# S5 output turned back in three parts, its input asked for one block earlier, and the squares of the second norm made per block

## The reference

```
u = rmsnorm(h);  z = u @ w_in                       # columns shared out to three mixers and gates
y_gla = (gated linear attention * silu(gate)) @ w_gla_out
s = per group of 16 channels: 64-dim complex state, associative scan over positions
s = gelu(C x + d * u);  s = s * sigmoid(s @ w_glu)   # S5 mixer: the "gated unit"
y_s5  = (s * silu(s_gate)) @ w_s5_out
y_att = (sliding-window attention * silu(a_gate)) @ w_attn_out
h = h + (g0*y_gla + g1*y_s5 + g2*y_att) @ w_out      # g = sigmoid(merge gates of u)
```

## Time and profile before

| | us |
|---|---|
| three timed runs | 1935.65, 1940.91, 1940.92 |
| profiled execution | 1936.7 (span of its trace 1934.8) |
| PE busy | 1774.6 (92%) |
| DVE busy | 969.9 (50%) |
| POOL busy | 782.0 (40%) |
| ACT busy | 694.5 (36%) |

### The profile page before, as it was taken

The page is one execution under the profiler, slowest core; times in us unless marked ns, Lnnn a source line. Parts: engine busy times, 40 slices in busy tenths (PEclk is TensorE's granted clock), DMA queues, the critical chain, the costliest instruction groups (busy, mean ns, idle before and its releaser), DMA issues.

```text
span 1934.8 us, 29460 instructions
## 1 busy us (share of the span) xinstructions
PE 1774.6 (92%) x12239; PEld 1588.4 (82%) x12239; DVE 969.9 (50%) x1527; ACT 694.5 (36%) x1236; POOL 782.0 (40%) x478
## 2 busy tenths in 40 slices
PE   6976898999998997989998999989999899799997
PEld 5876798999988996988997977777788687678886
DVE  8996134333429882467653203533333698635223
ACT  3453432444533221332324543344455221223322
POOL 2644665333323322533331786544332322334442
PEclk8898999999999998999998999999999999999999
DMA  9455244222254544535552333532223655523432
GB/s 146 142 164 152 79 104 117 81 68 66 65 146 142 181 138 100 104 82 177 157 163 85 99 87 88 132 93 77 76 61 72 176 172 179 110 77 98 140 101 87
DMA packets 356043, 221.77 MB, mean 115 GB/s; under 512 B 49604, under 2 KB 346744, under 8 KB 353352
## 3 DMA queue, kind: packets, MB, share of 16 engines
q1 hardware_dynamic: 345384, 189.75, 37.5%
q10 hardware_dynamic: 10528, 30.15, 4.6%
HBM read 172.17 MB, written 38.50 MB: 109 GB/s over the span
## 4 chain that ended last, share of the span: by engine, by line
PE 63%; DVE 10%; DMA 8%; POOL 6%; SPq 6%; ACT 4%; issue 3%; ACTq 0%; DVEq 0%; POOLq 0%
PE ring L794 45%; DMA sb_w_raw<-in_w_in 4%; POOL sb_w_lo L650 3%; PE ring L775 3%; PE ring L753 2%; PE aux L1037 2%; PE aux L1129 2%; DVE sb_s_prod L1515 1%; DVE sb_s_mat_prod L1515 1%; SPq L559 1%; DMA sb_w_raw<-in_w_s_out 1%; PE aux L1116 1%; SPq L525 1%; SPq L606 1%; DVE sb_s_gelu_lo L1515 1%
## 5 line engine op out<-in xcount | busy, mean ns | idle before, releaser
L650 POOL TENSOR_TENSOR sb_w_lo<-sb_w_raw,sb_w_hi 128x1024 fp32r<-128x1024 f32 x246 | 607.0, 2470 | 1067.3 <-ACT sb_w_hi L1181 1065.1
L1181 ACT ACTIVATE sb_w_hi<-sb_w_raw 128x1024 fp32r<-128x1024 f32 x246 | 259.9, 1057 | 654.5 <-DMA sb_w_raw<-in_w_in 409.6
L794 PE MATMUL ring<-sb_u_hi,sb_w_hi 128*128 128x264 f32 (+1 forms) x2112 | 358.7, 322 | 21.3 <-ACT sb_att_q L1223 11.0
L794 PEld LDWEIGHTS ring<-sb_u_hi,sb_w_hi 128*128 128x128 f32 x2112 | 304.8, 196 | 52.6 <-ACT sb_att_q L1223 12.6
L794 PE MATMUL ring<-sb_u_lo,sb_w_hi 128*128 128x264 f32 (+1 forms) x2112 | 338.4, 311 | 0.0
L794 PE MATMUL ring<-sb_u_hi,sb_w_lo 128*128 128x264 f32 (+1 forms) x2112 | 334.5, 309 | 0.0
L794 PEld LDWEIGHTS ring<-sb_u_lo,sb_w_hi 128*128 128x128 f32 x2112 | 298.5, 191 | 21.7
L794 PEld LDWEIGHTS ring<-sb_u_hi,sb_w_lo 128*128 128x128 f32 x2112 | 294.0, 188 | 21.1
L1213 ACT ACTIVATE sb_tmp_act<-ring 128x528 f32<-128x528 f32 (+1 forms) x112 | 67.5, 602 | 143.8 <-PE ring L794 103.3
L1437 ACT ACTIVATE sb_att_scores<-sb_att_scores,sb_att_neg_max 128x208 f32<-128x208 f32 x128 | 58.5, 458 | 90.8 <-DVE sb_att_neg_max L1800 90.8
L794 PE MATMUL ring<-sb_y_hi,sb_w_hi 128*128 128x264 f32 (+1 forms) x504 | 88.1, 325 | 3.2 <-ACT sb_w_hi L1181 3.1
(11 more groups left out here) (320 smaller groups left out, 2591.6 us busy)
## 6 DMA issues: line engine op xcount, KB each, us to landing
sb_w_raw<-in_w_in SPq DMA_DIRECT2D x166, 512.0 KB, 4.1
sb_s_loaded<-s_matrices ACTq DMA_DIRECT2D x16, 1808.0 KB, 7.5
s_matrices<-sb_s_phase SPq DMA_DIRECT2D x16, 528.0 KB, 3.2
s_matrices<-sb_s_mbt SPq DMA_DIRECT2D x16, 512.0 KB
s_matrices<-sb_s_ca SPq DMA_DIRECT2D x16, 512.0 KB
sb_w_raw<-in_w_gla_out SPq DMA_DIRECT2D x16, 512.0 KB, 4.1
sb_w_raw<-in_w_attn_out SPq DMA_DIRECT2D x16, 512.0 KB, 4.0
sb_w_raw<-in_s_w_glu SPq DMA_DIRECT2D x16, 512.0 KB, 4.2
```

Of the source, the lines that this page charges most:

```text
L650: pool.tensor_tensor(WL[:, w], WR[:, w], WH[:, w].bitcast(F32), ALU.subtract).then_inc(lo_ready, 1)
L794: last = pe.matmul(RING[:, 2 * r + hf, 0:c1 - c0], w[:, n % SLOTS, kt, :], moving(b[0], xx[:, kt], c0, c1), start=(term == 0 and kt == 0), ...
L1181: act.activation(WH[:, w], WR[:, w], ACT.Copy).then_inc(hi_ready, 1)
```

## The change

Four edits in one diff.

1. The S5 input is wanted behind block i = 2 instead of 3 (S5_IN = 2), and all 16 DMAs into Z4 are issued in SP's turn of ag 0. The scan of tile 0 moves up by one block with it. The places of the outputs, S5_OUT, keep their values.
2. The S5 output comes back in three parts, tiles 0 to 3, 4 and 5, 6 and 7, by 16 DMAs each, in SP's turns of i = 14, 18 and 21. Its target is a buffer of its own, YZ, in the room of the attention queries. ScalarE copies the first two parts in its turn of i = 20 and the third in that of i = 21; VectorE's subtractions follow in its turns of 21 and 22. GH moves to the room of Z. glu 0 runs alone (`project_as_made`), glu 1 by `project`.
3. The matrices of layer 1 lie elsewhere, and `input_matrix(1)` and `s5_matrices(1, 0)` are generators in two pieces each, run behind sg 2, 3, 4 and 5. The turn in which its C tiles are turned moves from sg 5 to sg 2.
4. In layer 0, ScalarE squares tile kt of the new h in the turn of wout kt + 1, into a buffer SQ of eight tiles in the room of UH. GpSimd adds tiles 1 to 6 to tile 0, behind its weight split of ga. TensorE sums that and tile 7 (`norm_sum_added`).

The core of the diff:

```diff
-S5_IN = 3
-S5_OUT = {S5_IN + 3 + 2 * j: j for j in range(KT)}
-S5_YT, S5_SPLIT = 21, 22
+S5_IN = 2
+S5_OUT = {6 + 2 * j: j for j in range(KT)}
+S5_YT = {14: (0, 4), 18: (4, 6), 21: (6, 8)}
+S5_SPLIT = {21: ((0, 4), (4, 6)), 22: ((6, 8),)}
+YT_PARTS = list(S5_YT.values())
...
-MATS_1 = [("sg", 5)] + [("ws5", j) for j in (0, 1, 2, 3, 5)] + [("wout", j) for j in (0, 2, 4)]
+MATS_1 = [("sg", 2)] + [("ws5", j) for j in (0, 1, 2, 3, 5)] + [("wout", j) for j in (0, 2, 4)]
...
-        GH = sb("s5_gelu_hi", [P, KT, L], F32R, at=[o_aq, o_aq + WIDE])
+        GH = sb("s5_gelu_hi", [P, KT, L], F32R, at=[base, base + WIDE])
+        YZ = sb("s5_out", [P, KT, STRIDE, STEPS], at=[o_aq, o_aq + WIDE])
...
-                    if name in (("ag", 0), ("ag", 1)):
-                        for q in (2 * name[1], 2 * name[1] + 1):
+                    if name == ("ag", 0):
+                        for q in range(QUADS):
...
-                    if name == S5F[S5_YT]:
-                        aux_read(sp, ly, ("y", 6))
-                        aux_read(sp, ly, ("y", 7))
+                    if name in S5F and S5F.index(name) in S5_YT:
+                        j0, j1 = S5_YT[S5F.index(name)]
+                        aux_read(sp, ly, ("y", j1 - 2))
+                        aux_read(sp, ly, ("y", j1 - 1))
                         for q in range(QUADS):
                             for t in range(STRIDE):
-                                sp.dma_start(Z[32 * q:32 * q + 32, :, t, :],
-                                             Z4[32 * t:32 * t + 32, :, q, :]).then_inc(yt_loaded, 16)
+                                sp.dma_start(YZ[32 * q:32 * q + 32, j0:j1, t, :],
+                                             Z4[32 * t:32 * t + 32, j0:j1, q, :]
+                                             ).then_inc(yt_loaded[YT_PARTS.index((j0, j1))], 16)
...
+                    if ly and b == 0:
+                        for kt in range(1, KT - 1):
+                            pool.wait_ge(sq_ready, KT + kt + 1)
+                            pool.tensor_tensor(SQ[:, 0], SQ[:, 0], SQ[:, kt], ALU.add).then_inc(sq_added, 1)
+                            pool.wait_ge(sq_added, kt)
...
+            def norm_sum_added(ly):
+                h = aux_take(ly, ("norm", 0))
+                for kt in (0, KT - 1):
+                    if kt:
+                        pe.wait_ge(sq_ready, KT * ly + KT)
+                    else:
+                        pe.wait_ge(sq_added, KT - 2)
+                    for hf, c0, c1 in column_parts(0):
+                        last = pe.matmul(AX_[:, 2 * h + hf, 0:c1 - c0], ONES[:], SQ[:, kt, c0:c1],
+                                         start=(kt == 0), stop=(kt == KT - 1))
+                last.then_inc(aux_full[h], 1)
...
-                project_two_as_made(ly, (("glu", 0), ("glu", 1)), GH, GL, ylo_ready, 32 * ly + 16)
-                for j in range(2, KT):
+                project_as_made(ly, ("glu", 0), GH, GL, ylo_ready, 32 * ly + 16)
+                for j in range(1, KT):
                     project(ly, ("glu", j), GH, GL)
...
+            def wout_squares(kt):
+                evacuated(act, 0, ("wout", kt))
+                act.activation(SQ[:, kt], H[:, kt], ACT.Square).then_inc(sq_ready, 1)
...
+                    if kind == "wout" and ly == 0 and j:
+                        wout_squares(j - 1)
...
-                            zs = [Z[:, j].rearrange("p s c -> p (s c)") for j in range(KT)]
-                            if i == S5_SPLIT:
-                                act.wait_ge(yt_loaded, 256 * ly + 256)
-                                for j in range(KT):
-                                    act.activation(GH[:, j], zs[j], ACT.Copy).then_inc(yhi_ready, 1)
+                            if i + 1 in S5_SPLIT:
+                                act.wait_ge(x_state, 8 * ly + 8)
+                                for part in S5_SPLIT[i + 1]:
+                                    act.wait_ge(yt_loaded[YT_PARTS.index(part)], 256 * ly + 256)
+                                    for j in range(*part):
+                                        act.activation(GH[:, j], YZ[:, j].rearrange("p s c -> p (s c)"), ACT.Copy
+                                                       ).then_inc(yhi_ready, 1)
...
-                    if ly == 0 and b == ("sg", 3):
-                        input_matrix(1)
+                    if ly == 0 and b == ("sg", 2):
+                        first_set = itertools.chain(input_matrix(1), s5_matrices(1, 0))
+                    if ly == 0 and kind == "sg" and 2 <= j <= 5:
+                        next(first_set)
...
-                            if i == S5_SPLIT:
-                                for t in range(KT):
+                            for part in S5_SPLIT.get(i, ()):
+                                for t in range(*part):
                                     dve.wait_ge(yhi_ready, 32 * ly + 16 + t + 1)
-                                    tt(GL[:, t], Z[:, t].rearrange("p s c -> p (s c)"), GH[:, t].bitcast(F32),
+                                    tt(GL[:, t], YZ[:, t].rearrange("p s c -> p (s c)"), GH[:, t].bitcast(F32),
                                        ALU.subtract).then_inc(ylo_ready, 1)
```

65 lines of the change are left out of this document (42 added, 23 removed).

## The result

The changed kernel takes 1917.61 us, median of four runs (1911.0 to 1920.78), the kernel before 1938.74 beside it (four runs): a ratio of 0.9891, 95% interval 0.9869 to 0.9912. That is 21 us of the 42 forecast, and outside the range on its slow side. The profiled execution took 1920.78 (span 1919.0), and TensorE is about as busy as before in less time (1778.7 us, 93%, by its page).

What follows compares the result with a forecast made beforehand. The prediction took the chain of waits as the bound, 63% of it on TensorE. A 12, B 27, C 1 and D 2 summed to 42 us off 1936.7, giving 1895 us, range 1878 to 1911.

Steps and rivals of the forecast that it cites:

- B: S5 output in three parts, glu 0 alone: TensorE's wait ahead of the gated unit shrinks; gain taken as 27 us.
- Cost nothing: Weight loads of blocks 17 and 21, behind the DMAs of parts 0 and 1, still reach TensorE in time: no loss.
- A: S5 input one block earlier: the first scan starts sooner and stalls at weights and first state go; taken 12 us.
- The new stall at ag 4's take: In layer 0, block 4's take, queued behind the first scan's second half, makes TensorE wait 3.6 us for block 6.
- its upper end: A with every VectorE operation at its undisturbed length: neither layer stalls, together a gain of 22 us.
- The second rival: In the first scan, block 4's take comes as late as the state did: A 0, gain 30, 1907 us; chance 0.10.
- the four subtractions in A's window: GpSimd's weight subtractions beside the first scan keep stretching VectorE's work, so the new stall of 3.6 us stays.
- C: First matrix set in four pieces behind sg 2 to 5: the stall is cut in two; gain taken as 1 us.
- D: Second norm with eight matmuls instead of 32, behind GpSimd's adds, ends earlier; gain taken as 2 us.
- The fourth rival: SP falls behind its weight loads at parts 0 and 1, stalling TensorE: slower, up to 1983 us; chance 0.07.

Runs made afterwards that it cites:

- b_off: The changed kernel with the S5 output moved by 16 DMAs at block 21 again and the first two gated unit blocks computed together: 1930.24 us, ratio 0.996.
- tanh_first: The changed kernel with ScalarE's tanh and y_hi in the turn of ag 1 ahead of the weight copy of ag 3: 1913.65 us, ratio 0.9879.
- half4_only: The changed kernel with the first scan's second half on VectorE behind the take of ag 4 instead of ag 3: 1914.31 us, ratio 0.9879.
- pool_small: The changed kernel with GpSimd subtracting only the first of eight pieces of each weight block in the S5 stage: 1883.84 us, ratio 0.9727.
- a_off: The changed kernel with 8 S5 input DMAs at ag 0 and 8 at ag 1 again, first state inputs behind ag 3: 1916.93 us, ratio 0.9896.
- cd_off: The changed kernel with the first matrix set behind sg 3 and sg 5 again and 32 matmuls in the second norm: 1917.56 us, ratio 0.9896.
- p01_adds: The changed kernel with output parts 0 and 1 behind their turn's weight load and four of GpSimd's six adds in wout: 1905.14 us, ratio 0.9831.

## Why the prediction was wrong, step by step

- **B, the waits: right.** Forecast a start after 2.2 us, measured 2.24, and 1.98 where 2.5 was forecast, behind GpSimd's rest of glu 0. The exact 2.2 is luck: the 16 issues took 10.65 us, 0.67 each, where I had taken 0.60, 1.05 us more in all, and the weights were split 4.7 us behind their issue (744.63 to 749.30) instead of 5.74, 1.1 less; layer 0's other two profiles have 1.69 and 2.84. The Trainium skill's rule on small transfers (DMA: Bandwidth & Descriptors, "Rules for kernel authors") gives no issue time, but it points the right way: a quarter of the bytes took the issue only from 0.72 to 0.67, and half of them (part 0, 11.35 us) to 0.71. Waits 22.7 of 23.0. The clock behind them: 2.6 in layer 1 (227.8 to 225.2), and in layer 0 2.2 (265.6 in b_off, with the wait, to 263.4 on the mean without), which rests on one profile. The granted clock fits: over the 14 us behind the wait it was 0.78 to 0.90 before, and is 1.00 in five of six cases now, 0.88 in the one below. 27.5, where I had taken 27.
- **B, "Cost nothing": the step that failed most, 11 us.** I asked only whether the delayed weights of blocks 17 and 21 reach TensorE in time. They did. But that sum had ScalarE's 1.1 us behind the load and no term for GpSimd's 2.4, nor for whom GpSimd meets. Its subtraction moved with the weights onto the second half of a scan, VectorE's products and the state's pair grew by 2.2 and 2.1 us in layer 0, and TensorE waited 2.82 and 3.07 for the last state and ran at a lower clock behind it: b_off against the changed kernel, 5.1 and 5.9 us.
- **A: 12 forecast, 4.5 to 5.5 measured.** The new stall at ag 4's take, 3.6 us in the sum for layer 0, came: 3.02, 1.76 and 5.85 us in the three profiles, 6.1 to 6.3 in layer 1. A stall at ag 3's take, which wasn't listed, stood beside it: 2.82, 2.77 and none, and 1.1 to 1.5. The chain's length was right: 21.1 us, and from 582.02 to 603.09 it took 21.1. Its start was not: I let VectorE begin 1.0 us behind block 2's end, though the earlier trace rows show ScalarE's turns held by late weights, and I hadn't counted the turn of ag 1. It was 4.0 us late (578.0 expected, shifted by the attention's end). The late start alone isn't the loss, as tanh_first takes 3.8 of it back and gains 0.0 and 1.5. The second half behind ag 4's take gives 1.9 and 2.8 by itself (half4_only), and cutting GpSimd's work to an eighth gives 8.8 and 10.1 (pool_small). So the order and the stretched operations kept A from its upper end. The second rival, "the new stall eats A", is what came for the most part.
- **Do A and B add?** In A's own part they do, as far as these profiles tell: 4.5 us gained with B in (three profiles against three), 4.8 without (b_off). By undoing A in the changed kernel it is 2.5. That a_off as a whole is only 1.2 us slower comes mostly from the clock behind the last state of layer 0, 1.00 against 0.50, 0.50 and 0.72 at the same wait, and no run shows that A has a hand in that. What A and B share is the neighbour: pool_small takes most of GpSimd's work away and gives 31 us of S5 stage back. The sentence on the Trainium skill's SBUF — State Buffer, "Who interferes with whom", was used for the four subtractions in A's window and nowhere else; the runs show it at the last scan as well, with 3.46 us for a pair of 1.32.
- **C: 1 forecast, 2 to 4 measured** (267.9 before to 265.6 in b_off, which has C; 267.5 in cd_off to 263.4), each against one profile, in a stretch that varies by 4: its size is open. Waits of 2.92 and 1.20 where I said about 4 and 1.5.
- **D: 2 forecast, nothing.** GpSimd's adds ended 5.6 us behind wout's last matmul where I had 4.7, and the eight matmuls, at a granted clock of 0.50, took 3.86, beyond my 3.5. So they ended 9.6 us behind wout, and the 32 of the kernel before, which started after 1.74, did so too. The granted clock there, and behind the waits of 2.82 and 2.24 (0.83 before, behind 14.2), by windows of the changed kernel, columns as above:

```profile
593.20:600.90 7.70, 7.62 (x48) 7.41 (x48) 7.61 (x7) 1.59 (x2) 2.38 (x1) 0.78 0.07 20
753.00:767.00 14.00, 13.95 (x102) 13.98 (x103) 1.06 (x2) 3.21 (x4) 6.21 (x3) 0.88 0.20 60
1024.50:1028.50 4.00, 3.86 (x8) 2.53 (x8) 0.03 (x1) 0.00 (x0) 2.35 (x1) 0.50 0.00 0
```

The sum with the measured terms: B's waits and clock 27.5, its side cost -11, A 5.5, C 2.3, D 0: 24.3, against 24.4 in the table. It closes by construction, since b_off splits the table's differences in two; it isn't a test of them. What is left to the 21 of the timed runs lies within their interval (17 to 25). The fourth rival named the right DMAs and the wrong victim.

## What to carry to other kernels

When a DMA is put ahead of a weight load, follow the load past the engine that needs it: to the engine that converts it, and to whoever shares memory access with that engine. A deadline met on TensorE says nothing on VectorE's. An edit that starts a chain earlier is worth what the first wait in the queues that feed the chain leaves of it; read that queue turn by turn. The earlier start still pays only as far as the engine behind it isn't held next: with tanh first, 3.8 us of it gave 0.0 and 1.5. And when an edit is undone alone, compare its own part of the trace before the whole: here 2.5 us of A were hidden by a clock that differed elsewhere.

## What the runs showed of the hardware

- One program's untouched thousand us differed by 16 from one execution to the next (998.5 and 1014.5, with a mean granted clock of 0.968 and 0.96 over the span). A single profile against a single one would have shown 9 us of loss that isn't there.
- The VectorE pair that makes a state took 1.32 us, and 3.34 to 3.52 in 21 cases of all profiles. In each of these a GpSimd subtraction of 2.3 to 2.9 us began within 0.6 us of its start, whichever scan it was in: it cost nearly the neighbour's whole length, not a share of it.
- After 5.75 us without work TensorE ran eight matmuls at a granted clock of 0.50, in 3.86 us (p01_adds: after 1.40 us, 2.02). In between the length of the wait didn't settle it: after 2.81 or 2.82 us for the last state of layer 0 the clock over the next 5.3 us was 0.50, 0.50 and 0.72 in three profiles of the changed kernel, and 1.00 in a_off and half4_only.
